# Differential attention of a transformer pair: the four raw-key projections spread over its 32 steps, and [high, low] values of 256 moving columns whose halves VectorE adds

## The chip, the cores and the metric

The kernel is one program on one NeuronCore of a Trainium2 chip, written with explicit semaphores for each engine: TensorE (PE), VectorE (DVE), ScalarE (ACT), GpSimd (POOL) and SyncE (SP). The metric is the device time of one execution in microseconds.

## The reference

Two transformer blocks over 512 tokens of width 1024 in float32. The first has a mixer and a gated feed-forward layer, the second a feed-forward layer, a mixer and another feed-forward layer. The change concerns the mixer of the second block, which has two branches over the same input `h @ w_in`:

```python
def diff_attention(q, k, v, cos, sin, lam_params, head_gain, lam_init):
    ...
        s = jnp.einsum('bqhcd,bkhcd->bhcqk', qb, k).astype(jnp.float32) * scale
        s = jnp.where(kpos[None, :] <= qpos[:, None], s, NEG_INF)
        p = jax.nn.softmax(s, axis=-1)
        a = p[:, :, 0] - lam * p[:, :, 1]
        return jnp.einsum('bhqk,bkhe->bqhe', a.astype(v.dtype), v)
    ...
    o = rmsnorm(o, head_gain) * (1.0 - lam_init)
```

with 8 heads of two 64-wide score maps and 128-wide values, and a sparse attention (`nsa`) with 16 query heads in two groups. It projects six key and value arrays. Two of them (`k_cmp`, `v_cmp`) are compressed: blocks of 32 tokens plus a position term go through a hidden layer of 256. The keys `k_slc` and `k_win` get a rotary embedding.

## The kernel before

Every float32 product is made of three passes: each operand is split into a high part (rounded to fp32r) and the rest, a low part, and `three` (L636 to L638) adds high x high, high x low and low x high in PSUM. Weights stream in 307 chunks of 128x1024 through six slots. SP loads a chunk into `raw`, ScalarE rounds it into `Wh` (L1210), VectorE subtracts for `Wl` (L1703): that pair is a *split*. It is issued five chunks ahead (`LEAD`). There are eight PSUM banks `ps[0]` to `ps[7]`, each with semaphores `full` and `free`; a table `STAGES` counts their uses in each stage. Every engine works its queue strictly in program order.

The stages around the change are, in this order: `vda` (value projection of the differential attention), `da` (the attention), `nsf` (four chunks, the feature-major projections of `k_cmp`, `v_cmp`, `k_slc` and `k_win`, called the raw keys here), `nst` (three chunks, the other values and the gates), `rope_q` (eight chunks) with the compression (`cmp`) between them, and `nsa`.

`da` has 32 steps t, four query tiles for each of 8 heads; the tile t % 4 sees (t % 4 + 1) x 128 keys. A step passes over four engines:
- TensorE `scores(t)` into two of the banks 0 to 3; VectorE `maxima(t)` (`nmx`); ScalarE `exps(t)` into `Pb` (L1371); VectorE `combine(t)`: `rr`, `gg` (L1907) and the difference of both maps in `Pb` (L1910).
- TensorE `turn(t)`: transposes into bank 4 or 5; ScalarE `high(t)` (`ATdh`, L1380); VectorE `low(t)` (`ATdl`, L1918).
- TensorE `values(t)`: for each of the t % 4 + 1 key blocks three matmuls of 128 moving columns, into bank 6 or 7 in turn; ScalarE `da_out(t)` scales it into `YD` (L1387) and frees the bank.

TensorE's order in step t is `values(t-2)`, `scores(t+2)`, `turn(t)`. ScalarE's is `da_out(t-3)`, `high(t)`, `exps(t+2)`, with the high parts of the head after the next between `high` and `exps` (V at t % 4 = 1, L1417; Q and K at t % 4 = 3, L1413). VectorE's is `combine(t)`, `low(t-1)`, `maxima(t+2)`. GpSimd subtracts for the low parts of Q, K and V (L510 to L520). The compression has two hidden layers, on TensorE in L1005, the first with weights `cw1k`, the second with `cw1v`; GpSimd makes their inputs `cA` (L566), and `cw1v` is loaded over the place of `YD` once that is stored in `y_dram`.

## Time and profile before

| | us |
|---|---|
| median of 3 runs | 2101.65 (2101.18 to 2110.67) |
| the profiled execution, its own time | 2101.01 |
| its span | 2099.2 |
| TensorE busy | 2016.0 (96%) |
| VectorE busy | 1042.3 (50%) |
| ScalarE busy | 814.6 (39%) |
| GpSimd busy | 276.5 (13%) |

The span lies inside the time; what is around it is 1.8 us. Busy time of TensorE holds modelled ends, so rates are read from the starts of matmuls. The stages stand at about 1124 to 1224 us (`da`), 1224 to 1246 (`nsf`), 1246 to 1259 (`nst`) and 1259 to 1340 (`rope_q` with the compression) from the start of the span.

### The profile page before, as it was taken

What the parts mean: (1) busy time and instruction counts of PE and PEld (TensorE: products, weight loads), DVE (VectorE), ACT (ScalarE), POOL (GpSimd) and SP (SyncE); (2) the same over time, 40 slices, a digit from 0 to 9 for tenths busy, and PEclk for the clock granted to TensorE, in tenths of its full rate; (3) what the DMA queues carried; (4) which work ended last, traced back from release to release, by engine and by line L of the source; (5) the groups of instructions that cost most, each with busy time, mean ns of one, the idle gap of its engine ahead of it and who ended that gap; (6) DMA issues with size and microseconds to landing.
All of it is one profiled execution on the core that took longest, in us unless ns stands there. A gap on an engine that the chain in (4) does not pass through costs nothing.

```text
span 2099.2 us, 25667 instructions
## 1 busy us (share of the span) xinstructions
PE 2016.0 (96%) x10244; PEld 1696.5 (81%) x10244; DVE 1042.3 (50%) x1606; ACT 814.6 (39%) x1482; POOL 276.5 (13%) x272
## 2 busy tenths in 40 slices
PE   6999999999999999999998899989899999999998
PEld 6887888888888888888887688777777888888887
DVE  5675565555353222335545766766565543222333
ACT  5442443333343222324225744455554333222322
POOL 1001000000000000000012432376763000000000
PEclk9999999999999999999998999999999999999999
DMA  5231233333223333332541043212115423332332
GB/s 192 81 101 61 100 102 101 92 99 101 92 90 102 99 100 92 99 101 81 151 130 41 1 171 120 90 31 61 46 37 180 126 80 105 96 101 92 99 100 71
DMA packets 58982, 200.13 MB, mean 95 GB/s; under 512 B 8080, under 2 KB 8112, under 8 KB 58480
## 3 DMA queue, kind: packets, MB, share of 16 engines
q1 hardware_dynamic: 53936, 178.29, 27.1%
q0 software_dynamic: 4928, 20.21, 2.7%
q8 instruction: 82, 1.34, 0.2%
q14 instruction: 36, 0.29, 0.0%
HBM read 181.16 MB, written 8.39 MB: 90 GB/s over the span
## 4 chain that ended last, share of the span: by engine, by line
PE 76%; DVE 7%; POOL 5%; ACT 5%; issue 3%; DVEq 2%; DMA 1%; POOLq 1%; SPq 0%; ACTq 0%
PE ps L636 24%; PE ps L637 24%; PE ps L638 24%; POOL PU L592 5%; DMA raw<-in_w_all 1%; DVE Wl L1703 1%; DVE XN L1743 1%; PE ps L1089 1%; DVEq L2262 1%; POOLq L581 1%; PE ps L1005 1%; ACT Pb L1371 1%; ACT Wh L1210 1%; DVE AUl L2267 1%; ACT PL L1466 1%
## 5 line engine op out<-in xcount | busy, mean ns | idle before, releaser
L1703 DVE TENSOR_TENSOR Wl<-raw,Wh 128x1024 fp32r<-128x1024 f32 x307 | 378.3, 1235 | 754.1 <-ACT Wh L1210 752.7
L636 PE MATMUL ps<-HTh,Wh 128*128 128x512 f32 (+1 forms) x1728 | 647.4, 375 | 8.9 <-DVE HTl L1752 7.0
L638 PE MATMUL ps<-HTh,Wl 128*128 128x512 f32 (+1 forms) x1728 | 641.9, 371 | 0.0
L637 PE MATMUL ps<-HTl,Wh 128*128 128x512 f32 (+1 forms) x1728 | 641.6, 371 | 0.0
L1210 ACT CAST Wh<-raw 128x1024 fp32r<-128x1024 f32 x307 | 322.0, 1051 | 782.5 <-DMA raw<-in_w_all 782.5
L636 PEld LDWEIGHTS ps<-HTh,Wh 128*128 128x128 f32 x1728 | 327.5, 190 | 64.7 <-issue 9.7
L638 PEld LDWEIGHTS ps<-HTh,Wl 128*128 128x128 f32 x1728 | 327.0, 189 | 56.1
L637 PEld LDWEIGHTS ps<-HTl,Wh 128*128 128x128 f32 x1728 | 327.3, 189 | 54.0
L636 PE MATMUL ps<-Wh,Yh 128*128 128x512 f32 x528 | 205.8, 390 | 0.0
L638 PE MATMUL ps<-Wh,Yl 128*128 128x512 f32 x528 | 205.5, 389 | 0.0
L637 PE MATMUL ps<-Wl,Yh 128*128 128x512 f32 x528 | 205.4, 389 | 0.0
L592 POOL TENSOR_SCALAR PU<-PU,ugg 128x512 f32<-128x512 f32 (+3 forms) x128 | 137.8, 1094 | 107.2 <-DVE ugg L2263 107.2
L636 PE MATMUL ps<-Wh,HTh 128*128 128x512 f32 (+2 forms) x320 | 119.1, 372 | 1.8 <-ACT qkr L1458 1.8
L637 PE MATMUL ps<-Wl,HTh 128*128 128x512 f32 (+2 forms) x320 | 118.1, 369 | 0.0
L638 PE MATMUL ps<-Wh,HTl 128*128 128x512 f32 (+2 forms) x320 | 118.1, 369 | 0.0
L638 PEld LDWEIGHTS ps<-Wh,Yl 128*128 128x128 f32 x528 | 99.1, 188 | 20.6
L636 PEld LDWEIGHTS ps<-Wh,Yh 128*128 128x128 f32 x528 | 99.1, 188 | 20.5
L637 PEld LDWEIGHTS ps<-Wl,Yh 128*128 128x128 f32 x528 | 99.1, 188 | 20.4
L1623 ACT ACTIVATE PU<-ps,umx 128x512 f32<-128x512 f32 (+3 forms) x128 | 65.7, 526 | 58.5 <-DVE umx L2255 58.5
L636 PEld LDWEIGHTS ps<-Wh,HTh 128*128 128x128 f32 x320 | 60.4, 189 | 12.0 <-ACT qkr L1458 2.2
L638 PEld LDWEIGHTS ps<-Wh,HTl 128*128 128x128 f32 x320 | 60.2, 188 | 10.1
L637 PEld LDWEIGHTS ps<-Wl,HTh 128*128 128x128 f32 x320 | 60.3, 188 | 9.7
(281 smaller groups left out, 2370.0 us busy)
## 6 DMA issues: line engine op xcount, KB each, us to landing
raw<-in_w_all SPq DMA_DIRECT2D x307, 512.0 KB, 3.5
swp_d<-qkd SPq DMA_DIRECT2D x64, 64.0 KB, 2.7
g_dram<-gst SPq DMA_DIRECT2D x16, 256.0 KB, 4.0
ring<-g_dram POOLq DMA_DIRECT2D x16, 256.0 KB, 3.5
gpre<-in_g_pre POOLq DMA_DIRECT2D x5, 512.0 KB, 3.8
X<-in_x SPq DMA_DIRECT2D x4, 512.0 KB, 5.0
swp_r<-qkr SPq DMA_DIRECT2D x16, 128.0 KB, 2.3
cw1k<-in_cw POOLq DMA_DIRECT2D x1, 2048.0 KB, 8.6
```

The source lines that it names most:

```text
L581: pool.drain()
L592: last = pool.tensor_scalar(p, p, ugg[:, s % 2, i:i + 1], None, ALU.mult)
L636: tensor.matmul(dst, a_hi, b_hi, start=start, stop=False)
L637: tensor.matmul(dst, a_hi, b_lo, start=False, stop=False)
L638: return tensor.matmul(dst, a_lo, b_hi, start=False, stop=stop)
L1005: last = tensor.matmul(ps[kv][:, ht * 64:ht * 64 + 62], cw[:, j, ht * P:(ht + 1) * P], cA[:, kv, j, :], start=j == 0, stop=j == 15)
L1089: return tensor.transpose(dst, p[:, a:a + P], ident[:])
L1210: scalar.copy(Wh[:, s, :], raw[:, s, :]).then_inc(w_hi, 1)
L1371: scalar.activation(Pb2[:, u, m, 0:w], ps[b][:, 0:w], ACT.Exp, bias=nmx[:, u, m:m + 1], accum_out=rs[:, u, m:m + 1]).then_inc(free[b], 1)
L1466: last = scalar.activation(PL[:, u, p:p + w], ps[b][:, o:o + w], ACT.Exp, bias=lmx[:, u, i:i + 1], accum_out=lsum[:, u, i:i + 1])
L1623: last = scalar.activation(PU[:, (s + 1) % 2, SCORE_AT[i]:SCORE_AT[i] + w], ps[b][:, o:o + w], ACT.Exp, bias=umx[:, s % 2, i:i + 1], accum ...
L1703: vector.tensor_tensor(Wl[:, s, :], raw[:, s, :], Wh[:, s, :], ALU.subtract).then_inc(w_lo, 1)
```

## The change

- The `nsf` stage is put ahead of `da` in the table, its 32 pieces (one `three` of 512 columns for each chunk and contraction tile) go into `da`: six ahead of the loop (`FIRST_STEPS`) and one behind `turn(t)` in the steps 0 to 25, all into bank 7. When a chunk is complete, at steps 2, 10, 18 and 26, ScalarE copies the bank (`nsf_out`) at the start of the step, and both engines make one weight split at the step's end.
- `Vst` holds the high and the low part of each key block side by side. `values` takes one matmul with 256 moving columns and one with 128 for each block, all into bank 6; the right half of the bank holds high x low. `da_out(t-2)` writes the left half to `YD`, and a new VectorE instruction `add_low(t-2)` adds the right half and frees the bank.
- The raw slice and window keys (`kraw`) and their swapped copy lie where the query tiles of finished heads were. Their swap DMAs are issued behind the last `nsf` chunk.
- TensorE no longer waits for all eight banks ahead of the loop.
- Behind the loop: squares and their reduction in two halves; the rotary work comes ahead of the head norms, and these come behind the low parts of the `nst` values. GpSimd loads `posT` and `cw1k` during `da`, makes both inputs in a row, and then stores `YD` and loads `cw1v`. The low part of the rotated keys (`ksl`) moves from c = 1 to c = 5 of `rope_q`.

```diff
-    ("da", 0, [0] * 8, [16, 16, 16, 16, 16, 16, 16, 16]),
-    ("nsf", 4, [1, 1, 1, 1, 0, 0, 0, 0], [0] * 8),
+    ("nsf", 4, [0, 0, 0, 0, 0, 0, 0, 4], [0] * 8),
+    ("da", 0, [0] * 8, [16, 16, 16, 16, 16, 16, 32, 0]),
...
-        Vst = at("Vst", -8, [P, 2, 2, SEQ], F32R)
+        Vst = at("Vst", -8, [P, 2, TT, 2, P], F32R)
...
-        DSQ = at("DSQ", 64, [P, TT, D])
+        DSQ = [at("DSQ0", 0, [P, 2, D]), at("DSQ1", 76, [P, 2, D])]
...
-        kraw = at("kraw", 44, [P, 2, SEQ])
...
+        kraw = at("kraw", 8, [P, 2, SEQ])
...
+        FIRST_STEPS = 6
+
+        def nsf_ends(t):
+
+            done = FIRST_STEPS + t
+            return done // 8 - 1 if done % 8 == 0 and 8 <= done <= 32 else None
...
-                c = m - CHUNK0["nsf"]
-                if c in (2, 3) and on("nsf"):
-                    swap("nsf", c - 2, c, 0, kraw[:, c - 2, :], swp_n[:, c - 2, :])
+                if m == CHUNK0["nsf"] + 3 and on("nsf"):
+                    for c in range(2):
+                        swap("nsf", c, 7, 2 + c, kraw[:, c, :], swp_n[:, c, :])
...
                 v_low(0, 7)
-
-                for b in (6, 7):
-                    pl.wait_ge(full[b], FILLED["nsf"][b])
+                if on("cmp"):
+                    pool.drain()
+                    load(posT[:], t["posT"], in_pos)
+                    load(cw1k[:].rearrange("p j n -> p (j n)"), t["cw1"][0], in_cw)
+
+                pl.wait_ge(full[6], FILLED["da"][6] + TOTAL)
...
-                for tt in range(TT):
-                    pl.wait_ge(da_fin, tt + 1)
-                    pl.dma_start(y_dram[tt], YD[:, tt, :]).then_inc(yd_out, 16)
                 def inputs(kv):
 
-                    pl.wait_ge(free[kv], FREED["nst"][kv])
+                    pl.wait_ge(free[7], FREED["nsf"][7] + kv + 1)
...
                 inputs(0)
+                load(w2k[:], t["w2k"], in_cw)
+                load(w2v[:], t["w2v"], in_cw)
+                inputs(1)
+                pool.drain()
+                for tt in range(TT):
+                    pl.wait_ge(da_fin, tt + 1)
+                    pl.dma_start(y_dram[tt], YD[:, tt, :]).then_inc(yd_out, 16)
                 pl.wait_ge(yd_out, 16 * TT)
                 load(cw1v[:].rearrange("p j n -> p (j n)"), t["cw1"][1], in_cwv)
-                inputs(1)
-                pool.drain()
...
             def values(t):
                 u, n = t % 2, t % 4 + 1
-                b = 6 + u
-                bank_free("da", b, t // 2)
+                b = 6
+                bank_free("da", b, t)
                 if t % 4 == 0:
                     pe.wait_ge(st_lo, 4 * (t // 4) + 4)
                 bank_free("da", 4 + u, t // 2 + 1)
                 for j in range(n):
                     a = slice(j * P, (j + 1) * P)
-                    last = three(ps[b][:, 0:P], ATdh[:, u, 0, a], ATdl[:, u, 0, a], Vst[:, t // 4 % 2, 0, a], Vst[:, t // 4 % 2, 1, a],
-                                 j == 0, j == n - 1)
+                    v = Vst[:, t // 4 % 2, j, :, :]
+                    tensor.matmul(ps[b][:, 0:2 * P], ATdh[:, u, 0, a], v.rearrange("p a n -> p (a n)"), start=j == 0, stop=False)
+                    last = tensor.matmul(ps[b][:, 0:P], ATdl[:, u, 0, a], v[:, 0, :], start=False, stop=j == n - 1)
                 last.then_inc(full[b], 1)
+
+            def nsf_steps(a, b):
+                for n in range(a, b):
+                    c, k = n // 8, n % 8
+                    w = weights(CHUNK0["nsf"] + c)
+                    if k == 0:
+                        bank_free("nsf", 7, c)
+                    q = slice(k * P, (k + 1) * P)
+                    last = three(ps[7][:], Wh[:, w, q], Wl[:, w, q], HTh[:, k, :], HTl[:, k, :], k == 0, k == KT - 1)
+                    if k == KT - 1:
+                        last.then_inc(w_used, 1)
 
             def attention():
                 scores(0)
                 scores(1)
+                nsf_steps(0, FIRST_STEPS)
                 for t in range(TOTAL):
                     if exists(t - 2):
                         values(t - 2)
                     if exists(t + 2):
                         scores(t + 2)
                     turn(t)
+                    if FIRST_STEPS + t < 32:
+                        nsf_steps(FIRST_STEPS + t, FIRST_STEPS + t + 1)
                 values(TOTAL - 2)
                 values(TOTAL - 1)
...
-                for b in range(8):
-                    pe.wait_ge(free[b], FREED["da"][b])
...
-            if on("nsf"):
-                for c in range(4):
-                    gemm_f("nsf", c, c)
...
             def da_out(t):
-                u = t % 2
-
-                if t >= TOTAL - 2:
-                    filled("da", 6 + u, t // 2)
-                scalar.activation(YD[:, t % 4, span(0, 2 * P, t // 4 * P, P)], ps[6 + u][:, 0:P], ACT.Copy,
-                                  scale=rr[:, t % STEPS, 0:1]).then_inc(free[6 + u], 1)
+                filled("da", 6, t)
+                scalar.activation(YD[:, t % 4, span(0, 2 * P, t // 4 * P, P)], ps[6][:, 0:P], ACT.Copy,
+                                  scale=rr[:, t % STEPS, 0:1]).then_inc(y_part, 1)
+
+            def nsf_out(c):
+                chunk_done("nsf", c)
+                if c >= 2:
+                    ac.wait_ge(st_lo, 4 * (4, 7)[c - 2] + 2)
+                dst = kcv[:, c, :] if c < 2 else kraw[:, c - 2, :]
+                scalar.copy(dst, ps[7][:]).then_inc(free[7], 1)
 
             def attention():
                 exps(0)
+                high_parts(0, 0, 1)
                 exps(1)
+                high_parts(0, 1, 0)
                 for t in range(TOTAL):
-                    if exists(t - 3):
-                        da_out(t - 3)
+                    if nsf_ends(t) is not None:
+                        nsf_out(nsf_ends(t))
+                    if exists(t - 2):
+                        da_out(t - 2)
                     high(t)
                     if t % 4 == 1 and exists(t + 4):
                         high_parts(0, t // 4 + 1, 1)
...
                         high_parts(0, t // 4 + 2, 0)
                     if exists(t + 2):
                         exps(t + 2)
-                for t in range(TOTAL - 3, TOTAL):
-                    da_out(t)
+                    if nsf_ends(t) is not None:
+                        split(CHUNK0["nsf"] + nsf_ends(t) + LEAD)
+                da_out(TOTAL - 2)
+                da_out(TOTAL - 1)
...
             if on("nsf"):
 
-                scalar.drain()
-                scalar.activation(DSQ[:], YD[:], ACT.Square).then_inc(da_sq, 1)
-                ac.wait_ge(da_ss, 1)
+                ac.wait_ge(free[6], FREED["da"][6] + TOTAL)
+                for n in range(2):
+                    scalar.activation(DSQ[n][:], YD[:, 2 * n:2 * n + 2, :], ACT.Square).then_inc(da_sq, 1)
+                split(CHUNK0["nst"] + LEAD)
+                ac.wait_ge(da_ss, 2)
                 scalar.activation(hsd[:], hss[:], ACT.Sqrt, scale=1.0 / P, bias=eps[:]).then_inc(da_sd, 1)
-                for c in range(4):
-                    split(CHUNK0["nsf"] + c + LEAD)
-                    chunk_done("nsf", c)
-                    dst = kcv[:, c, :] if c < 2 else kraw[:, c - 2, :]
-                    scalar.copy(dst, ps[c][:]).then_inc(free[c], 1)
             if on("nst"):
-                for c in range(3):
-                    split(CHUNK0["nst"] + c + LEAD)
+                split(CHUNK0["nst"] + 1 + LEAD)
                 chunk_done("nst", 2)
                 for tt in range(TT):
                     for m in range(2):
                         scalar.copy(vhl[m][:, tt, :, 0:HD], ps[tt][:, m * P:(m + 1) * P].rearrange("p (g d) -> p g d", g=2))
                 for tt in range(TT):
                     scalar.activation(gates[:, tt, :], ps[tt][:, 2 * P:VG_W], ACT.Sigmoid).then_inc(vs_hi, 1)
+                split(CHUNK0["nst"] + 2 + LEAD)
...
+            def add_low(t):
+
+                ve.wait_ge(y_part, t + 1)
+                y = YD[:, t % 4, span(0, 2 * P, t // 4 * P, P)]
+                vector.scalar_tensor_tensor(out=y, in0=ps[6][:, P:2 * P], scalar=rr[:, t % STEPS, 0:1], in1=y,
+                                            op0=ALU.mult, op1=ALU.add).then_inc(free[6], 1)
+
             def attention():
                 maxima(0)
                 maxima(1)
...
                     combine(t)
                     if exists(t - 1):
                         low(t - 1)
+                    if exists(t - 2):
+                        add_low(t - 2)
                     if exists(t + 2):
                         maxima(t + 2)
+                    if nsf_ends(t) is not None:
+                        split(CHUNK0["nsf"] + nsf_ends(t) + LEAD)
                 low(TOTAL - 1)
+                add_low(TOTAL - 2)
+                add_low(TOTAL - 1)
...
             if on("nsf"):
-                ve.wait_ge(da_sq, 1)
-                vector.tensor_reduce(hss[:], DSQ[:].rearrange("p i (h d) -> p (i h) d", d=P), AX.X, ALU.add).then_inc(da_ss, 1)
-                ve.wait_ge(da_sd, 1)
-                vector.reciprocal(hrs[:], hsd[:])
-                vector.drain()
-                for i in range(TT):
-                    r = hrs[:, i * 8:(i + 1) * 8].rearrange("p (h a) -> p h a", a=1).broadcast_to((P, 8, P))
-                    blk = YD[:, i, :].rearrange("p (h d) -> p h d", d=P)
-                    vector.tensor_tensor(blk, blk, r, ALU.mult).then_inc(da_fin, 1)
-                for c in range(4):
-                    split(CHUNK0["nsf"] + c + LEAD)
+                for n in range(2):
+                    ve.wait_ge(da_sq, n + 1)
+                    vector.tensor_reduce(hss[:, 16 * n:16 * n + 16], DSQ[n][:].rearrange("p i (h d) -> p (i h) d", d=P), AX.X,
+                                         ALU.add).then_inc(da_ss, 1)
+                split(CHUNK0["nst"] + LEAD)
                 ve.wait_ge(in_rope, 64)
 
                 def keys_out(kind):
...
                     last.then_inc(roped, 1)
 
                 keys_out(0)
-                split(CHUNK0["nst"] + LEAD)
+                ve.wait_ge(da_sd, 1)
+                vector.reciprocal(hrs[:], hsd[:])
+                vector.drain()
                 split(CHUNK0["nst"] + 1 + LEAD)
                 keys_out(1)
                 vector.drain().then_inc(ks_f, 1)
             if on("nst"):
-                split(CHUNK0["nst"] + 2 + LEAD)
                 for tt in range(TT):
                     ve.wait_ge(vs_hi, tt + 1)
                     for m in range(2):
                         last = vector.tensor_tensor(vhl[m][:, tt, :, HD:P], ps[tt][:, m * P:(m + 1) * P].rearrange("p (g d) -> p g d", g=2),
                                                     vhl[m][:, tt, :, 0:HD], ALU.subtract)
                     last.then_inc(free[tt], 1)
+                split(CHUNK0["nst"] + 2 + LEAD)
+                for i in range(TT):
+                    r = hrs[:, i * 8:(i + 1) * 8].rearrange("p (h a) -> p h a", a=1).broadcast_to((P, 8, P))
+                    blk = YD[:, i, :].rearrange("p (h d) -> p h d", d=P)
+                    vector.tensor_tensor(blk, blk, r, ALU.mult).then_inc(da_fin, 1)
```

Three places show how the queues change. In the rows `ps` is a bank, `Pb` the exponentials, `ATdh` and `ATdl` the two parts of the transposed weights.

TensorE, step 4, `values(2)` and the piece ahead of it; before:

```order
L789 MATMUL ps<-ident,Pb_90 128x128 x4
L636 MATMUL ps<-Vst,ATdh 128x128
L637 MATMUL ps<-Vst,ATdh 128x128
L638 MATMUL ps<-Vst,ATdl 128x128
L636 MATMUL ps<-Vst,ATdh 128x128
L637 MATMUL ps<-Vst,ATdh 128x128
L638 MATMUL ps<-Vst,ATdl 128x128
L636 MATMUL ps<-Vst,ATdh 128x128
L637 MATMUL ps<-Vst,ATdh 128x128
L638 MATMUL ps<-Vst,ATdl 128x128
```

and with the change:

```order
L795 MATMUL ps<-ident,Pb_90 128x128 x4
L642 MATMUL ps<-HTh,Wh 128x512
L643 MATMUL ps<-HTl,Wh 128x512
L644 MATMUL ps<-HTh,Wl 128x512
L808 MATMUL ps<-Vst,ATdh 128x256
L809 MATMUL ps<-Vst,ATdl 128x128
L808 MATMUL ps<-Vst,ATdh 128x256
L809 MATMUL ps<-Vst,ATdl 128x128
L808 MATMUL ps<-Vst,ATdh 128x256
L809 MATMUL ps<-Vst,ATdl 128x128
```

The third matmul of each block went into the first, and a piece of `nsf` stands between the transposes and the values.

ScalarE, step 10, where the second chunk ends; before:

```order
L1387 ACTIVATE YD<-ps,rr 128x128
L1380 CAST ATdh<-ps 128x384
L1371 ACTIVATE Pb_90,rs<-ps,nmx 128x128 x2
L1387 ACTIVATE YD<-ps,rr 128x128
L1380 CAST ATdh<-ps 128x512
```

and with the change:

```order
L1409 COPY kcv<-ps 128x512
L1401 ACTIVATE YD<-ps,rr 128x128
L1397 CAST ATdh<-ps 128x384
L1388 ACTIVATE Pb_90,rs<-ps,nmx 128x128 x2
L1227 CAST Wh<-raw 128x1024
L1401 ACTIVATE YD<-ps,rr 128x128
L1397 CAST ATdh<-ps 128x512
```

`YD` is now the output of step 8, not 7; the copy stands ahead of it, and a split behind the exponentials.

VectorE, the same step; before:

```order
L1905 RECIPROCAL rr<-rs 128x2
L1907 SCALAR_TENSOR_TENSOR gg<-rs,nlam,rr 128x1
L1910 SCALAR_TENSOR_TENSOR Pb_90<-Pb_90,gg 128x384
L1918 TENSOR_TENSOR ATdl<-ps,ATdh 128x256
L1897 TENSOR_REDUCE nmx<-ps 128x1 x2
```

and with the change:

```order
L1929 RECIPROCAL rr<-rs 128x2
L1931 SCALAR_TENSOR_TENSOR gg<-rs,nlam,rr 128x1
L1934 SCALAR_TENSOR_TENSOR Pb_90<-Pb_90,gg 128x384
L1942 TENSOR_TENSOR ATdl<-ps,ATdh 128x256
L1948 SCALAR_TENSOR_TENSOR YD<-ps,rr,YD 128x128
L1921 TENSOR_REDUCE nmx<-ps 128x1 x2
L1727 TENSOR_TENSOR Wl<-raw,Wh 128x1024
```

The addition into `YD` stands ahead of the maxima, the split behind them.

## Rows read from the trace of the kernel before

**Rows 1.** The page: busy time of each engine over the span.

```profile
PE 2016.0 (96%) x10244; PEld 1696.5 (81%) x10244; DVE 1042.3 (50%) x1606; ACT 814.6 (39%) x1482; POOL 276.5 (13%) x272
```

**Rows 2.** Windows: stretch, its length, busy of each engine, PEclk, DMA share, GB/s.

```profile
1124.00:1126.00 2.00, 1.68 (x9) 1.71 (x9) 0.29 (x1) 1.95 (x4) 1.37 (x2) 0.51 0.01 2
...
1160.00:1172.00 12.00, 9.77 (x75) 8.17 (x74) 8.84 (x24) 8.95 (x30) 5.79 (x4) 1.00 0.01 3
```

**Rows 3.** Timeline of TensorE, last value projection to first score.

```profile
1124.32 0.44 PE L636 MATMUL ps<-Kst,Qst 128*128 128x128 f32 x1 [3.38 <-DVE vd L2122]
```

**Rows 4.** Timeline of VectorE: combines at 1136 and 1219, one turn between.

```profile
1136.37 0.15 DVE L1905 RECIPROCAL rr<-rs 128x2 f32<-128x2 f32 x1
...
1159.55 0.15 DVE L1905 RECIPROCAL rr<-rs 128x2 f32<-128x2 f32 x1
...
1161.51 0.17 DVE L1905 RECIPROCAL rr<-rs 128x2 f32<-128x2 f32 x1
...
1163.94 0.15 DVE L1905 RECIPROCAL rr<-rs 128x2 f32<-128x2 f32 x1
...
1167.44 0.17 DVE L1905 RECIPROCAL rr<-rs 128x2 f32<-128x2 f32 x1 [0.60 <-ACT Pb L1371]
...
1170.07 1.51 DVE L1897 TENSOR_REDUCE nmx<-ps 128x1 f32<-128x512 f32 x2 [1.38 <-PE ps L781]
...
1171.50 0.15 DVE L1905 RECIPROCAL rr<-rs 128x2 f32<-128x2 f32 x1
...
1219.19 0.17 DVE L1905 RECIPROCAL rr<-rs 128x2 f32<-128x2 f32 x1
```

**Rows 5.** Timeline of ScalarE in the same turn.

```profile
1164.04 0.58 ACT L1380 CAST ATdh<-ps 128x512 fp32r<-128x512 f32 x1 [1.04 <-PE ps L789]
...
1166.33 0.47 ACT L1371 ACTIVATE Pb<-ps,nmx 128x256 f32<-128x256 f32 x1
...
1167.24 0.36 ACT L1387 ACTIVATE YD<-ps,rr 128x128 f32<-128x128 f32 x1
```

**Rows 6.** Timeline of TensorE in the same turn.

```profile
1162.61 0.28 PE L637 MATMUL ps<-Kst,Qst 128*128 128x256 f32 x1
...
1162.73 0.28 PE L638 MATMUL ps<-Kst,Qst 128*128 128x256 f32 x1
...
1163.39 0.61 PE L789 MATMUL ps<-ident,Pb 128*128 128x128 f32 x4
...
1168.38 0.28 PE L636 MATMUL ps<-Vst,ATdh 128*128 128x128 f32 x1
...
1168.49 0.28 PE L637 MATMUL ps<-Vst,ATdh 128*128 128x128 f32 x1
```

**Rows 7.** Timelines of VectorE and GpSimd at the same instant.

```profile
1133.75 1.28 DVE L1907 SCALAR_TENSOR_TENSOR gg<-rs,nlam,rr 128x1 f32<-128x1 f32 x1
1133.75 1.26 POOL L520 TENSOR_TENSOR Vst<-vd,Vst 128x512 fp32r<-128x512 f32 x1 [3.70 <-ACT Vst L1417]
```

**Rows 8.** Timeline of TensorE: first `nsf` and first `nst` matmul.

```profile
1224.04 0.44 PE L636 MATMUL ps<-HTh,Wh 128*128 128x512 f32 x1
...
1245.90 0.30 PE L636 MATMUL ps<-Wh,HTh 128*128 128x304 f32 x1
```

**Rows 9.** Timelines of ScalarE and VectorE: the two halves of one split.

```profile
1241.54 1.05 ACT L1210 CAST Wh<-raw 128x1024 fp32r<-128x1024 f32 x1 [2.78 <-DMA raw<-in_w_all]
...
1242.63 1.23 DVE L1703 TENSOR_TENSOR Wl<-raw,Wh 128x1024 fp32r<-128x1024 f32 x1 [2.13 <-ACT Wh L1210]
```

**Rows 10.** Timelines of VectorE and GpSimd after the attention.

```profile
1228.35 4.42 DVE L2127 TENSOR_REDUCE hss<-DSQ 128x32 f32<-128x4096 f32 x1 [5.82 <-ACT DSQ L1552]
...
1247.71 8.88 POOL L566 TENSOR_TENSOR cA<-kcv,posT 64x248 f32<-64x248 f32 x8 [8.67 <-issue]
```

**Rows 11.** The chain that ended last: start, length, what.

```profile
1270.37 7.09 PE ps L1005 x64
...
1293.40 7.14 PE ps L1005 x64
```

44 lines of the change are left out of this document (21 added, 23 removed).

## The prediction

> **What bounds the kernel now.** I read the page first: TensorE is busy for 96% of the span [rows 1], so a change pays by what it takes out of TensorE's stream or out of its waits. Next the windows and the timelines of the differential attention (1124 to 1224 us). Here TensorE is not the bound. The work goes in 32 steps, one for each query tile of each head; four steps, one head, I call a turn. A turn in the middle of the stage takes 1171.50 - 1159.55 = 11.95 us (third tile to third tile), and the seven turns from the `combine` of the first head's fourth tile to that of the last head take 1219.19 - 1136.37 = 82.8 us [rows 4]. TensorE is busy for 9.77 of 12 us [rows 2]. VectorE waits for ScalarE's exponentials (0.60) and for scores (1.38), ScalarE for transposes (1.04) [rows 4, 5]: a ring of short waits over three engines. After it TensorE runs dense: the four chunks of `nsf` take 1245.90 - 1224.04 = 21.9 us [rows 8].
>
> **What the change removes.** All 96 `nsf` matmuls leave the stretch behind the attention: -21.9 us, if they fit into TensorE's gaps there. By matmul starts, a 128-column matmul costs 0.11 (1168.38 to 1168.49) and a 256-column one 0.12 (1162.61 to 1162.73) [rows 6]; so a [high, low] pair in one matmul saves 0.10 to 0.11 for each of 80 blocks, about 8.5 us of TensorE. Per turn TensorE is busy for 9.77 us at most [rows 2], some of that modelled tails. Less 1.0 (ten blocks), plus four `nsf` steps of 21.9/32 = 0.68, that is 11.5 or less: it still fits into 11.95. Trainium skill, "TensorE: Matmul & The Clock Gate", section "Back-to-back issue gap", gives N/2.4 + 2.5 ns, that is 56 and 109 ns, and by it the pair would save 3 ns; the rows' 0.11 at 128 columns speaks against this. By the page a TensorE-bound loop would gain 8 us less; my sum has another bound and would stay.
>
> **The new loop, one turn.** VectorE gets four adds (`add_low`; I take 0.30 each, between a 128-column multiply-add from SBUF, 0.27, and a 128-column subtraction from PSUM, 0.28, plus a semaphore). ScalarE's order changes: `da_out(t-2)` now waits for the values of its own step, and VectorE's `add_low` behind it stands ahead of `maxima(t+2)`. Take 0 as the start of `combine` of the fourth tile.
> (a) Transposes at 1.35 (before: 1.88, 1163.39 [rows 6]). ScalarE's `high` 0.65 later, at 2.0; then 0.48 for it and 1.81 for the Q and K casts (1164.04 to 1166.33 is 2.29), 0.91 for the exponentials (1166.33 to 1167.24) [rows 5]: 5.2. `da_out`, 0.36: 5.6.
> (b) VectorE is there earlier: 2.43 (1161.51 to 1163.94 [rows 4]) + 0.28 + 1.46 for the next `combine` and `low` = 4.2. It waits 1.4 us. Then add 0.3 and maxima over 384 columns (1.43 for 512; I take 1.15): the next `combine` at 7.05, where it is 5.93 (1167.44) before [rows 4].
> (c) Values of the fourth tile need that add (one output bank now instead of two), start at 5.95, take 1.0; scores follow; the maxima over 512 columns start at 8.6 and take 1.43 (1170.07 to 1171.50): `combine` at 10.05, before 9.99 [rows 4]. So far nothing is lost.
> (d) ScalarE casts V at 9.26, GpSimd takes its low part from 9.96 to 11.2. VectorE's `gg` comes 0.23 into its `combine`, at 10.28, while that runs. The one place before where both start together shows `gg` at 1.28 us instead of 0.22, as long as GpSimd's 1.26 [rows 7]: an instruction with two SBUF inputs waits for GpSimd. In the middle turns of before VectorE is just ahead of it and GpSimd is the one that waits. Here VectorE loses 0.8 to 0.9. (Trainium skill, "GPSIMD Engine Reference", section "Specifications": SBUF interfaces are shared with VectorE for instructions with two SBUF inputs. By that rule the wait comes again in each turn, as the trace has it.)
> (e) `low` ends at 12.4; add 0.3, maxima over 128 columns 0.57: the next turn begins at 13.3, not 11.95: +1.35. Without (d) it is 12.4, since the exponentials end at 11.1 and `da_out` at 11.5.
> (f) At steps 2, 10, 18 and 26 a chunk ends. ScalarE adds a copy (0.5, [rows 5] has 0.58 for a 128x512 cast) and, behind the exponentials of step t+2, a split of 1.05; VectorE's half, 1.23, waits for it [rows 9]. Exponentials can begin at 13.0 after the first maximum, end 13.75; split to 14.8, VectorE's half to 16.05. Such a turn costs 16.05, that is 2.75 more. The cover is TensorE's own work, which is shorter.
> (g) From step 3 to step 31 there are three turns of 13.3, three of 16.05, and a last one without Q, K and V casts, 10.35 (VectorE's own work; before 9.89): 98.4 us, before 82.8. So +15.6.
>
> **Its start and end.** TensorE starts a score at 1124.32 after waiting 3.38 us for the last of VectorE's V copies [rows 3]; the change waits for each bank alone, so it starts when the first of four copies of 0.6 is done, 2.4 earlier, at 1121.95. But six `nsf` steps (4.1 us) now stand ahead of `scores(2)`, which VectorE's queue needs: second `combine` at 1129.9, third 1132.6, hit by (d), then the first split: fourth at 1138.8, before 1136.37 [rows 4]. +2.4. From the last `combine` to the last value it is 4.65 (before 1224.04 - 1219.19 = 4.85): -0.2.
>
> **Behind the attention.** T is the new end, 1136.37 + 2.4 + 98.4 + 4.65 = 1241.85. TensorE gets to the first hidden layer (cw1k) at T + 24.5 and to the second (cw1v) at T + 47.5, as 1270.37 and 1293.40 lie to 1245.90 [rows 8, 11]. VectorE: squares by ScalarE end T + 4.8 (halves of 3.63), reduction in two halves (4.42 in one [rows 10]) T + 7.4, split T + 9, keys 7 us under GpSimd's work T + 16, split, second keys T + 23, first bank free T + 23.5. One us of margin: I charge 0.5. GpSimd: a drain ahead of its first input instruction waits for loads in flight (8.67 us before [rows 10]), here the two rope loads, T + 5; two input stages of 8.9 [rows 10] and two loads between them: T + 26.5. VectorE's four head norms (as many elements as the 4.42 us reduction; I take 4.6) end at T + 31; y_dram lands 6.6 later and cw1v 8.5 after that, by the trace's median landing times of the same loads: T + 46.2, hidden by about 1 us. What is late next when the margin is gone is cw1v, 1 us for 1 us. The swap DMAs of the keys now sit in SP's queue behind the load for step 26, long before they are needed; rope_q swaps need `roped` 25 and 26, T + 16 and T + 23, and block only a load that isn't wanted before T + 40. The ksl subtraction (2.28) moves to c = 5, into 1.1 us of idle before `cmp_shift(1)` and 0.7 of the second score half: nothing.
>
> **Sum.** -21.9 (nsf) + 2.4 (start) + 15.6 (turns) - 0.2 (end) + 0.5 (bank) = -3.6. The profiled execution took 2101.0 us (span 2099.2), 0.65 under the median of 2101.65. 2101.0 - 3.6 = 2097.4; I say 2097.5.
>
> **Rivals.** (A) The forecast, gain of the overlap eaten by the longer turns: 2092 to 2101, chance 0.5.
> (B) The turns keep the length of before, and only the splits lengthen them by VectorE's own 1.2: T = 1138.0 + 82.8 + 3.6 + 4.65 = 1229, that is 2084. If VectorE's work alone bounds (11.95 less 0.60, 1.38 and 0.23 of waits, plus 1.2 for the adds, and 1.2 per split), T is near 1222 and the time 2077. For it: that idle time [rows 4]. Against: the waits in (b) and (f) come out of queue order, not load. Chance 0.17.
> (C) Collisions as in (d) do not happen, because the V cast falls elsewhere: 7 x 0.9 less, 2091. Chance 0.1, half of it under 2091.
> (D) The other side: GpSimd's Q and K lows (three instructions of 1.27 us from 3.2 on) also hit `combine` of the first two tiles. In my schedule these hide behind the 1.4 us wait of (b). If that wait is under 0.5 us, each turn pays 0.8 to 1.3: +6 to +9, 2103 to 2106. Chance 0.13.
> (E) The granted clock. Behind the 3.38 us of idle it stood at 0.51 [rows 2], 1.2 instead of 2.4 GHz. The change leaves 1.2 us of idle there and dense work behind it, so I expect 1.0. If it falls anyway, the six steps cost 4 us more and each further us at the low level up to 0.5: 2102 to 2113. Chance 0.07.
> (F) cw1v or the keys are late by several us: 2100 to 2105, chance 0.03.
>
> **How the numbers follow.** What a measurement here can tell from no change is about 0.5%, 10.5 us: faster is below 2091.1. Faster: all of B, half of C and a little of A = 0.24. Slower, above 2112.2: the tail of E and D, 0.03. Same: 0.73. The range leaves out the lower half of B and the upper end of E: 2084 to 2106. Unknown costs lie in it: an add of 0.25 or 0.4 (32 x 0.05 to 0.1, 2 to 3 us), (d) between 0 and 1.27 per turn (-6 to +3).
>
> **What the new profile would show.** `nst` starts at 1242 (right: 1237 to 1247; B right: before 1230). `combine` of a fourth tile to the next: 13.3 and, with a chunk's end, 16.0. VectorE idle before `add_low`, released by ScalarE's YD, near 1.4 per turn, and before the split's Wl near 2. `gg` of third tiles at about 1 us. PEclk 1.0 throughout the attention. No TensorE wait at the first hidden layer over 1 us. The prediction is wrong if ScalarE gets to `da_out` before VectorE asks for it, or if TensorE waits for cw1v.

## The result

The changed kernel takes 2117.8 us (median; 2116.3 to 2120.2, 7 runs), the kernel before 2101.65: a ratio of 1.0066 (95% interval 1.0051 to 1.0081), 0.66% slower. The forecast was 2097.5, with 2084 to 2106 as its range. It was wrong in sign and size. Single executions of the kernel before go from 2100.9 to 2110.7 us and those of the changed one from 2116.3 to 2120.2, so the two don't overlap. The profiled execution has a span of 2116.0 us where that of before has 2099.2: 16.8 us to find.

The page of the changed kernel says little. TensorE is busy 10 us longer than in [rows 1] with 80 instructions fewer, so part of its work ran slower; PEclk in 40 slices of 53 us shows where:

```profile
PE 2026.0 (96%) x10164; PEld 1704.8 (81%) x10164; DVE 1052.2 (50%) x1639; ACT 816.1 (39%) x1483; POOL 275.2 (13%) x272
...
PEclk9999999999999999999999987999999999999999
```

**The attention came out near the forecast, in part by luck.** VectorE's timeline of one turn with a split; the reciprocals are `combine`'s first instruction, as in [rows 4]:

```profile
1157.22 0.35 DVE L1948 SCALAR_TENSOR_TENSOR YD<-ps,rr,YD 128x128 f32<-128x128 f32 x1 [1.58 <-ACT YD L1401]
...
1161.23 0.15 DVE L1929 RECIPROCAL rr<-rs 128x2 f32<-128x2 f32 x1
...
1161.74 1.57 DVE L1934 SCALAR_TENSOR_TENSOR Pb<-Pb,gg 128x384 f32<-128x384 f32 x1
...
1166.12 1.23 DVE L1727 TENSOR_TENSOR Wl<-raw,Wh 128x1024 fp32r<-128x1024 f32 x1 [1.68 <-ACT Wh L1227]
1167.26 0.16 DVE L1929 RECIPROCAL rr<-rs 128x2 f32<-128x2 f32 x1
```

One line shows the wait of (b): before its add into `YD` VectorE stood 1.58 us for ScalarE's `da_out`. (d) is there too, but it fell on `Pb`, 1.57 us where the same form elsewhere takes 0.62, and only in three of the six turns that prepare a V: in the other three GpSimd's instruction was the one that took longer (1.71 us instead of 1.27). Before its half of the split (`Wl`) it stood 1.68 us for ScalarE's half. The eight fourth-tile combines are at 1138.63, 1151.59, 1167.26, 1181.84, 1197.51, 1210.52, 1226.17 and 1237.84: 99.2 us where 98.4 were forecast. Single turns were off by -0.4 to +1.3 us, and the errors partly cancelled.

Two things of the attention were missed: TensorE waits up to 2.98 us for `Pb` behind a split, and its granted clock falls behind such waits. Timeline, then windows (PEclk is the third number from the end):

```profile
1168.96 1.12 PE L795 MATMUL ps<-ident,Pb 128*128 128x128 f32 x4 [2.98 <-DVE Pb L1934]
```

```profile
1160.00:1170.00 10.00, 5.96 (x41) 5.18 (x40) 7.62 (x18) 5.39 (x15) 1.27 (x1) 0.91 0.20 56
1170.00:1180.00 10.00, 10.00 (x52) 8.18 (x50) 6.37 (x18) 6.65 (x18) 4.22 (x4) 0.75 0.00 0
```

Even so TensorE reached the first hidden layer at 1269.80, ahead of the 1270.37 of [rows 11], and did not wait there. **All of the loss, and 0.6 us more, lies behind that point.** What TensorE did from 1284 on, in its timeline:

```profile
1287.97 0.39 PE L644 MATMUL ps<-HTh,Wl 128*128 128x512 f32 x1
1293.87 7.09 PE L1051 MATMUL ps<-kcb,qn 128*128 128x64 f32 x32 [5.51 <-ACT qn L1608]
1300.75 13.86 PE L1021 MATMUL ps<-cA,cw1v 128*128 128x62 f32 x64
```

It stood 5.51 us for ScalarE's `qn` (`query(3)`), where the kernel before stands 0.69:

```profile
1289.62 3.79 PE L1035 MATMUL ps<-kcb,qn 128*128 128x64 f32 x32 [0.69 <-ACT qn L1585]
```

Then the 32 matmuls of `cmp_scores(0)` took 7.1 us (before: 3.8) and the second hidden layer 13.6 from its start to the next stage (before: 7.1). The clock was at its lower level, 1.2 GHz (PEclk 0.50):

```profile
1284.00:1290.00 6.00, 4.36 (x20) 3.25 (x18) 0.00 (x0) 0.00 (x0) 0.00 (x0) 1.00 0.91 365
1292.00:1316.00 24.00, 22.13 (x100) 21.84 (x101) 7.12 (x10) 6.44 (x7) 0.60 (x1) 0.50 0.10 27
```

ScalarE's timeline says what held `query(3)`, and the DMA issues say why (line, queue, count, KB of one, median us to landing):

```profile
1282.96 0.41 ACT L1603 COPY kcb<-ps 64x62 f32<-64x62 f32 x2
1292.15 1.04 ACT L1227 CAST Wh<-raw 128x1024 fp32r<-128x1024 f32 x1 [8.78 <-DMA raw<-in_w_all]
1293.22 0.60 ACT L1608 ACTIVATE qn<-ps 128x512 f32<-128x512 f32 x1
```

```profile
1281.98 0.54 POOL L471 DMA_DIRECT2D cw1v<-in_cw  x1 [6.71 <-DMA y_dram<-YD]
```

```profile
1282.46 0.33 SPq L450 DMA_DIRECT2D raw<-in_w_all  x1
```

```profile
cw1v<-in_cw POOLq DMA_DIRECT2D x1, 2048.0 KB, 9.7
raw<-in_w_all SPq DMA_DIRECT2D x2, 512.0 KB, 7.7
```

ScalarE's order is split, then query. The split waited 8.78 us for a weight chunk, issued at 1282.46 and used at 1292.15, 9.7 us later; the page's median landing of a chunk is 3.5. GpSimd had issued the 2 MB load of cw1v half a microsecond ahead of it, at 1281.98, after 6.71 us for the stores of YD. The DMA share from 1284 to 1290 is 0.91. The kernel before has cw1v issued at 1256.55. Its ScalarE waits for the same chunk too, but 3.47 us:

```profile
1287.41 1.05 ACT L1210 CAST Wh<-raw 128x1024 fp32r<-128x1024 f32 x1 [3.47 <-DMA raw<-in_w_all]
1288.97 0.60 ACT L1585 ACTIVATE qn<-ps 128x512 f32<-128x512 f32 x1 [0.51 <-PE ps L638]
```

Its query then still waits 0.51 us for TensorE: half a microsecond was all the margin of that queue, and I had not looked at it. By the starts of TensorE's rows up to 1340, the changed kernel loses 4.8 us by the longer wait, 3.3 and 6.5 us in the two slow stages, and 1.9 in the first projection matmuls behind them, at 0.43 instead of 0.23: 16.4. About 1 us more is lost behind 1500 us, where its clock is below 1.0 for longer than that of before.

### The profile page after: what moved, and what is told of

Read it like the earlier page. It is cut to its first block, busy times and chain, and to the rows that moved or that the text cites. A ratio compares the mean times of both kernels' runs of the same rounds, so it can differ in the third digit from the quotient of the medians.

```text
span 2116.0 us, 25539 instructions
## 1 busy us (share of the span) xinstructions
PE 2026.0 (96%) x10164; PEld 1704.8 (81%) x10164; DVE 1052.2 (50%) x1639; ACT 816.1 (39%) x1483; POOL 275.2 (13%) x272
## 3 DMA queue, kind: packets, MB, share of 16 engines
q8 instruction: 81, 1.33, 0.2%
## 4 chain that ended last, share of the span: by engine, by line
PE 75%; DVE 7%; POOL 5%; ACT 5%; issue 3%; DVEq 2%; DMA 2%; POOLq 1%; SPq 0%; ACTq 0%
PE ps L642 23%; PE ps L644 23%; PE ps L643 23%; POOL PU L598 5%; DMA raw<-in_w_all 2%; PE ps L1021 1%; DVE XN L1767 1%; ACT Wh L1227 1%; PE ps L1105 1%; DVE Wl L1727 1%; DVEq L2300 1%; ACT XN L1260 1%; POOLq L587 1%; DVE AUl L2305 1%; ACT PL L1495 1%
```

## The experiments

Theory 1: a chain. cw1v slows a chunk, ScalarE's split waits, `query(3)` is queued behind it, TensorE waits, its clock falls. Every ratio below is to the kernel before, whose median on the chips of these runs was 2104.4 to 2105.9 us.

### query_first: query ahead of the split from c = 3 on

```diff
                 for c in range(8):
-                    split(CHUNK0["rope_q"] + c + LEAD)
+                    if c < 3:
+                        split(CHUNK0["rope_q"] + c + LEAD)
                     query(c)
+                    if c >= 3:
+                        split(CHUNK0["rope_q"] + c + LEAD)
```

> The changed kernel (2117.8 us), with one move on ScalarE: from query(3) on, query(c) stands ahead of the split of the weight chunk and no longer behind it. No engine does more or less. Theory 1 (the loss of 16 us is a chain: the 2 MB load of cw1v slows a weight chunk from 3.5-4.3 to 9.67 us, ScalarE's split waits for it, query(3) is queued behind, TensorE stands 5.5 us and its clock then stays at half until 1318): the load still overlaps the chunk and the chunk still takes over 8 us, but the wait of TensorE ahead of cmp_scores(0) falls from 5.51 to under 1.5 us, the clock stays at 1.0, hidden layer 2 starts by 1293 instead of 1300.95, and the kernel takes 2100 to 2103 us. Rival A (TensorE would only wait later, at hidden layer 2 for cw1v itself, which lands at 1291.7): a wait of 3 to 5 us there, clock down again, 2110 to 2115. Rival B (the loss has its root in the attention, where the clock fell already): no change, 2116 to 2119.

2107.4 us, ratio 1.0016 (0.9999 to 1.0032): 5 of 6.6 thousandths regained, not all, and more than the 2100 to 2103 us expected. The wait is 0.69 us, the second hidden layer starts at 1292.5: the chain up to there is as theory 1 has it. But a new wait stands at the next attention:

```profile
1336.30 0.79 PE L1094 MATMUL ps<-ksh,QSn 128*128 128x512 f32 x1 [3.84 <-ACT PU L1650]
```

```profile
1306.99 1.23 DVE L1730 TENSOR_TENSOR Wl<-raw,Wh 128x1024 fp32r<-128x1024 f32 x1 [6.29 <-ACT Wh L1227]
...
1333.32 1.19 DVE L2239 TENSOR_TENSOR CS<-CS,cst 128x992 f32<-128x992 f32 x1
```

VectorE's half of a split now waits 6.29 us for ScalarE's half behind `query(4)`, and VectorE's later work, the scores' shift that ScalarE's exps need, comes 5 us later (1333.32, in query3 below 1328.15; 1.9 us of that is a head start that query3's execution has since the attention). I had moved the queue's mistake from one engine to another.

### filled_gap: TensorE kept busy in the gap

```diff
                 rope_q(3)
+                bank_free("cmpa", 3)
+                for n in range(24):
+                    tensor.matmul(ps[3][:], HTh[:, n % 8, 0:P], HTh[:, n % 8, :], start=True, stop=True)
                 pe.wait_ge(free[7], FREED["rope_q"][7] + 2)
```

> The changed kernel with 24 matmuls of 512 columns more on TensorE behind rope_q(3), whose results nobody reads (bank 3 is free there). They fill the 5.5 us for which TensorE waits; ScalarE's order, the load and the chunk stay. It parts the wait from the clock. Theory 1 says that of the loss of 16 to 17 us the wait itself is 4.8 and the halved clock behind it 11 to 12: with the gap filled the clock stays at 1.0, cmp_scores(0) takes 3.8 and hidden layer 2 takes 7.1 us as in the kernel before, and the kernel takes 2105 to 2108 us. Rival C (the clock falls because of what ran before the gap, or the load, and not because of the gap): the clock is at half all the same and the kernel takes 2116 to 2121.

2104.8 us, ratio 1.0003 (0.9989 to 1.0017). The forecast of theory 1 was 2105 to 2108. The chunk was as late as before, and idle work alone gave back 13 us (1 us of it, by the traces, is a head start that this execution has at the first hidden layer):

```profile
1291.46 1.05 ACT L1230 CAST Wh<-raw 128x1024 fp32r<-128x1024 f32 x1 [9.14 <-DMA raw<-in_w_all]
```

```profile
1293.00:1304.00 11.00, 10.81 (x97) 10.81 (x97) 6.46 (x9) 3.73 (x4) 0.00 (x0) 1.00 0.10 25
```

The granted clock stayed at 1.00, and rival C falls. So of the loss the larger part is the clock, not the wait.

### no_transfer: without cw1v's load

The load is left out, and the second hidden layer takes the weights of the first.

```diff
-                load(cw1v[:].rearrange("p j n -> p (j n)"), t["cw1"][1], in_cwv)
...
-                    cw = (cw1k, cw1v)[kv]
+                    cw = cw1k
```

> The changed kernel without the load of cw1v: hidden layer 2 uses cw1k instead and waits for the stores of YD alone, so its values are not the reference's. Theory 1: the weight chunk that took 9.67 us takes 3.5 to 4.5, ScalarE's split and query(3) come 5 us earlier, TensorE waits under 1 us, the clock stays at 1.0, and the kernel takes 2100 to 2103 us, the same as with query(3) ahead. Rival D (the chunk is slow for another reason, such as being requested late): the chunk still takes over 7 us and the time stays at 2112 to 2119.

2110.4 us, ratio 1.0013 (0.9990 to 1.0035). ScalarE's wait for the chunk fell from 8.78 to 4.38 us and TensorE's from 5.51 to 1.11: the chunk lands 5.3 us after its issue instead of 9.7, so the load is what slows it (rival D falls; 3.5 to 4.5 had been expected). But behind a wait of 1.11 us the clock fell all the same and stood at 0.50 from 1291 to 1311 in this execution:

```profile
1288.85 5.21 PE L1050 MATMUL ps<-kcb,qn 128*128 128x64 f32 x32 [1.11 <-ACT qn L1607]
```

```profile
1287.13 1.05 ACT L1226 CAST Wh<-raw 128x1024 fp32r<-128x1024 f32 x1 [4.38 <-DMA raw<-in_w_all]
```

The time expected of it, 2100 to 2103, was missed by the median and by the profiled run (2109.1 us of span). The ten runs lie in two groups: four at 2100.4 to 2103.0, as expected, and six at 2110.4 to 2113.8. In the profiled one, of the second group, TensorE takes 9.7 us more than before from `cmp_scores(0)` to `cmp_scores(1)`. That the first group are the executions in which the clock holds would fit, but none of them was profiled.

### norms_early: stores and cw1v earlier

The four products are also taken out behind the lows of `vhl`.

```diff
                 vector.reciprocal(hrs[:], hsd[:])
                 vector.drain()
+                for i in range(TT):
+                    ...
+                    vector.tensor_tensor(blk, blk, r, ALU.mult).then_inc(da_fin, 1)
```

> The changed kernel with VectorE's four products of the head norms put back ahead of the keys (as the kernel before has them) instead of behind the lows of vhl. YD is stored and cw1v loaded some 10 us earlier (issue by 1272 instead of 1281.98). Theory 1: the load falls on another chunk, one that no queue is waiting for; TensorE's wait at cmp_scores(0) falls below 1.5 us and the clock holds; but the norms (4 x 1.1 us) now delay the keys and the vhl lows, which may cost TensorE up to 3 us at the first hidden layer: 2100 to 2106 us. Rival E (wherever the load lies it hits the chunk that ScalarE waits for, since a chunk is asked for every 3 us): a wait of 3 to 5 us appears at an earlier chunk, 2110 to 2118.

2114.1 us, ratio 1.0048 (1.0028 to 1.0067). The norms moved the wait to VectorE's side: TensorE stood at the first hidden layer for the lows of `vhl`, and the layer took 13.3 us:

```profile
1271.62 13.27 PE L1021 MATMUL ps<-cA,cw1k 128*128 128x62 f32 x64 [3.77 <-DVE vhl L2196]
```

cw1v was issued at 1278.66, only 3.3 us earlier, since the stores wait on GpSimd behind `inputs(1)`; the issue by 1272 that I expected did not come. At `cmp_scores(0)` the wait was 0.69. The time lies in the range of rival E, but by another path than E's: the wait is for VectorE, as theory 1 had allowed with up to 3 us, and no chunk was in flight beside cw1v. So this run says little on where the load could stand.

### query3: the one query that matters

```diff
-                    split(CHUNK0["rope_q"] + c + LEAD)
-                    query(c)
+                    if c == 3:
+                        query(c)
+                        split(CHUNK0["rope_q"] + c + LEAD)
+                    else:
+                        split(CHUNK0["rope_q"] + c + LEAD)
+                        query(c)
```

> As query_first, but only query(3) stands ahead of its split; for query(4) to query(7) the split is ahead again. In query_first the wait at cmp_scores(0) was gone (0.7 us, clock 1.0, hidden layer 2 at 1292.5), and a new one of 3.8 us stood at the first scores of the next attention (1331 to 1335), after which the clock was at half. Theory 1 with this added (a split that waits for its chunk delays whatever stands behind it; the moved splits now stood ahead of the next attention's exps): that wait goes back to 0.6 us, no fall of the clock up to 1344, and the kernel takes 2098 to 2101 us, no more than the kernel before. Rival F (the wait at 1331 comes from elsewhere in the changed kernel, such as the later keys): it stays, and the time is that of query_first, 2105 to 2108.

2103.8 us, ratio 1.0003 (0.9991 to 1.0014). Two instructions exchanged give back the 0.66%. `cw1v` still takes 9.4 us, the chunk beside it 8.1, and ScalarE still waits for it, but the query is no longer behind it:

```profile
1287.01 3.79 PE L1051 MATMUL ps<-kcb,qn 128*128 128x64 f32 x32 [0.69 <-ACT qn L1608]
```

```profile
1286.36 0.60 ACT L1608 ACTIVATE qn<-ps 128x512 f32<-128x512 f32 x1 [5.03 <-PE ps L644]
1288.58 1.04 ACT L1227 CAST Wh<-raw 128x1024 fp32r<-128x1024 f32 x1 [1.62 <-DMA raw<-in_w_all]
```

The time is 3 us over what I expected; the kernel before, on these chips, is 3 us over its first median too. Theory 1 stands: with the chain cut, the changed kernel equals the one before. One thing doesn't add up in the medians: filled_gap keeps the wait of 4.8 us and query3 doesn't, yet both measure 1.0003. The traces say more. query3 is 2.6 us ahead of before at 1322 and until 1530; then its clock falls where that of before doesn't, at a wait of the same length, and it ends level. First query3, then before, TensorE and its windows:

```profile
1533.24 2.40 PE L1105 MATMUL ps<-ident,PU 128*128 128x128 f32 x10 [3.36 <-POOL PU L598]
1530.00:1545.00 15.00, 11.76 (x59) 9.84 (x59) 6.12 (x15) 7.08 (x23) 9.33 (x10) 0.77 0.13 39
```

```profile
1535.32 1.31 PE L1089 MATMUL ps<-ident,PU 128*128 128x128 f32 x10 [3.35 <-POOL PU L592]
1530.00:1545.00 15.00, 11.50 (x73) 9.47 (x72) 8.05 (x21) 7.53 (x23) 11.11 (x11) 1.00 0.18 47
```

Now the question is the one that the forecast answered with -3.6: where do the 21.9 us go that leave the stretch behind the attention?

### query3_lag: the split's halves in different steps

```diff
 ScalarE
-                    if nsf_ends(t) is not None:
-                        split(CHUNK0["nsf"] + nsf_ends(t) + LEAD)
+                    if nsf_ends(t - 1) is not None:
+                        split(CHUNK0["nsf"] + nsf_ends(t - 1) + LEAD)
 VectorE
-                    if nsf_ends(t) is not None:
-                        split(CHUNK0["nsf"] + nsf_ends(t) + LEAD)
+                    if nsf_ends(t - 2) is not None:
+                        split(CHUNK0["nsf"] + nsf_ends(t - 2) + LEAD)
```

> query3, and in the attention each split of a weight chunk stands one step later on ScalarE and two steps later on VectorE, so that VectorE never waits for ScalarE's half of it. In the changed kernel the turns with a split took 15.67 us against 13.0, and the split itself is only 1.05 and 1.23 us; TensorE stood 2.98 us and its clock fell. Theory 2 (the split's excess over its 1.2 us is the two engines' halves in one step, and the gap that drops the clock): split turns take 14.2 to 14.8, four of them save 4 to 6 us, and the kernel takes 2093 to 2097 us. Rival G (the halves are cheap and what is slow in a turn is the chain exps, da_out, add_low, maxima): under 1.5 us, 2097 to 2100.

2096.2 us, ratio 0.9968 (0.9951 to 0.9985). Turns with a split take 14.4 us (1164.91 to 1179.28; the first 14.5), the others 13.0; the last combine is at 1231.78, in query3 at 1235.81. Time and turns are as theory 2 has them. VectorE's waits ahead of `Wl` in the loop (6.9 us in query3) are gone, TensorE's longest for `Pb` from 3.0 to 1.8, and PEclk was 1.00 from 1120 to 1220. A split now costs a turn 1.4 us more, near VectorE's own 1.2 for it.

### old_values and old_values_lag: values as in the kernel before

```diff
-                    tensor.matmul(ps[b][:, 0:2 * P], ATdh[:, u, 0, a], v.rearrange("p a n -> p (a n)"), start=j == 0, stop=False)
-                    last = tensor.matmul(ps[b][:, 0:P], ATdl[:, u, 0, a], v[:, 0, :], start=False, stop=j == n - 1)
+                    last = three(ps[b][:, 0:P], ATdh[:, u, 0, a], ATdl[:, u, 0, a], v[:, 0, :], v[:, 1, :], j == 0, j == n - 1)
...
-                    if exists(t - 2):
-                        add_low(t - 2)
```

> query3 with the values as three products of 128 columns, as in the kernel before: ScalarE's da_out frees the bank and VectorE adds no halves; the key projections stay inside the attention, the values' bank stays single. It undoes one part of the change. Per head that gives VectorE back four add_low (0.3 us each and their waits, 16.6 us in 15 over the loop) and costs TensorE ten matmuls of 0.11 us. Theory 3 (VectorE's add_low and its wait for da_out, queued behind ScalarE's exps, set the turn): the loop's 99.2 us fall by 6 to 12, and the kernel takes 2088 to 2094 us. Rival H (TensorE's own work sets the turn, since the projections take their place in it): the added 8.8 us of matmuls take it back, 2098 to 2104.

> old_values and the later splits together. By theory 2 and 3 the two savings add but for 1 to 2 us: 2084 to 2091. If the turn is then set by TensorE's own work (rival H), the later splits give under 2 us on top of old_values.

old_values: 2100.5 us, ratio 0.9993 (0.9972 to 1.0014). From the first to the last of the fourth-tile combines it takes 95.1 us, query3 98.0: 2.9 us less, not 6 to 12. The time is in the range of rival H, but what held it wasn't TensorE's work alone: VectorE's waits for `da_out` (15.2 us in 13 over query3's loop) became waits for scores (16.7 us in 14) and for ScalarE's half of the splits (10.4 us in 4; 6.9 in query3). With the splits apart (old_values_lag) it pays: 2088.8 us, 0.9918 (0.9900 to 0.9935) in 4 runs, against 0.9968 of query3_lag, combines in steps of 12.1 and 14.8 us, the last at 1228.04.

### values_alone: the other part, on the kernel before

```diff
-                    last = three(ps[b][:, 0:P], ATdh[:, u, 0, a], ATdl[:, u, 0, a], Vst[:, t // 4 % 2, 0, a], Vst[:, t // 4 % 2, 1, a],
-                                 j == 0, j == n - 1)
+                    v = Vst[:, t // 4 % 2, j, :, :]
+                    tensor.matmul(ps[b][:, 0:2 * P], ATdh[:, u, 0, a], v.rearrange("p a n -> p (a n)"), start=j == 0, stop=False)
+                    last = tensor.matmul(ps[b][:, 0:P], ATdl[:, u, 0, a], v[:, 0, :], start=False, stop=j == n - 1)
...
+                    if exists(t - 3):
+                        add_low(t - 3)
```

> The kernel before with one part of the change alone: values as 256 and 128 moving columns, the right half added by VectorE at step t-3, two banks as before; the key projections stay behind the attention. TensorE saves ten matmuls per head; VectorE gains four add_low of 0.34 us per head. Theory 3 (VectorE and ScalarE set the turn, TensorE does not): the saved matmuls buy nothing and each turn of 11.95 us grows by 0.3 to 1.4 us, 2 to 11 us over eight heads: 2104 to 2113 us where the kernel before has 2102 to 2105. Rival H (TensorE's work sets the turn): the turn falls by up to 1 us, 2094 to 2101.

2111.5 us, ratio 1.0030 (1.0019 to 1.0041). Its seven turns take 1225.95 - 1135.05 = 90.9 us, in [rows 4] 82.8: the part costs 8 us, though it takes 8 us of matmuls out of TensorE. Waits of the attention (us in all, times, longest):

```profile
PE ps L789 <- DVE Pb L1912: 14.4, 9, 1.9
DVE YD L1926 <- ACT YD L1388: 13.0, 8, 2.3
PE ps L802 <- DVE YD L1926: 10.8, 8, 2.0
```

In the kernel before TensorE waits 6.6 us for `Pb` and 9.0 for the values' banks, and VectorE has no add to wait for. The part is a loss by itself. It costs 8 us here, 5 thousandths in query3_lag and 1 thousandth, within the noise, in query3, where VectorE's waits for the split's other half took its place.

### nst_early, scores_first and nst_early_filled: more out of the end

On top of old_values_lag, the first `nst` chunk goes into the attention's end, then scores ahead of values, then (on nst_early alone) ten idle matmuls ahead of the first hidden layer:

```diff
 nst_early
+                nst_tiles(0, (0, 1))
                 values(TOTAL - 2)
+                nst_tiles(0, (2, 3))
                 values(TOTAL - 1)
 scores_first
-                    if exists(t - 2):
-                        values(t - 2)
                     if exists(t + 2):
                         scores(t + 2)
+                    if exists(t - 2):
+                        values(t - 2)
 nst_early_filled
                 rope_q(1)
+                bank_free("cmpa", 4)
+                for n in range(10):
+                    tensor.matmul(ps[4][:], HTh[:, n % 8, 0:P], HTh[:, n % 8, :], start=True, stop=True)
                 cmp_hidden(0)
```

> old_values_lag with the first chunk of the next projection (nst, 36 matmuls of 304 columns, 5 us, banks 0 to 3, which the last exps have freed) inside the attention's end: tiles 0 and 1 ahead of values(30), tiles 2 and 3 ahead of values(31). There TensorE stood some 2 us in waits and ran at half clock from 1229 to 1240. Theory 4 (the end of the attention is a gap that costs itself and the clock behind it; work that is ready fills it): the first hidden layer starts 3 to 6 us earlier than in old_values_lag (1261.8), clock 1.0 at 1230 to 1240, 2083 to 2087 us. Rival I (behind the attention VectorE's reductions, splits and lows set the time, not TensorE): the first hidden layer waits for the lows of vhl or cm_a as much longer, under 1 us gained.

> nst_early with scores(t + 2) ahead of values(t - 2) on TensorE. In old_values_lag VectorE's maxima wait 13.8 us over the loop for scores, which stand behind the values. If that wait sits in the turn's chain (scores, maxima, exps, da_out, high), the loop shortens by 3 to 8 us: 2076 to 2083. Rival J (da_out and with it the values' bank then come later, and what was saved at the maxima is lost at values): within 1.5 us of nst_early, or slower.

> nst_early with ten matmuls of 512 columns more on TensorE ahead of the first hidden layer, whose results nobody reads (bank 4): they last about the 2.25 us for which TensorE there waits for the lows of vhl. In nst_early the first hidden layer started 3.6 us earlier than in old_values_lag but took 10.9 us in place of 6.9, and at the next attention all was lost (1322.9 against 1320.0). Theory 5 (what is won ahead of a wait is lost because the wait halves the clock behind it; the wait itself loses nothing): the first hidden layer starts at 1258 to 1259 and takes 7.0 us, the clock holds, the next attention starts at 1315 to 1317, 2084 to 2088 us. Rival K (what stands behind, the stores of YD, cw1v or the chunks, then sets the time): a wait of over 1 us turns up at the second hidden layer or at cmp_scores(0), clock down there, 2091 to 2097.

nst_early 2096.5 us (0.9965, 0.9949 to 0.9981), scores_first 2097.2 (0.9968, 0.9952 to 0.9985), nst_early_filled 2100.7 (0.9979, 0.9967 to 0.9990): all three worse than the 2088.8 they build on. In scores_first the loop took 89.9 us instead of nst_early's 91.0, not 3 to 8 less, and the time is the same (rival J). TensorE's timelines of nst_early and of nst_early_filled:

```profile
1258.17 11.37 PE L1026 MATMUL ps<-cA,cw1k 128*128 128x62 f32 x64 [2.25 <-DVE vhl L2197]
```

```profile
1258.24 7.33 PE L1026 MATMUL ps<-cA,cw1k 128*128 128x62 f32 x64 [0.58 <-DVE vhl L2200]
...
1283.54 13.42 PE L1026 MATMUL ps<-cA,cw1v 128*128 128x62 f32 x64 [2.02 <-DMA cw1v<-in_cw]
```

In nst_early the layer starts 3.6 us earlier than in old_values_lag, after 2.25 us of wait for VectorE's lows (rival I), and takes 10.9 us at a falling clock. The wait is one that the edit made: `values(31)` now stands behind the tiles, ScalarE's last `da_out` and the squares behind it come 4.9 us later than in best_again (the last section of these), and VectorE's lows end at 1259.2 instead of 1256.4. ScalarE, first nst_early, then best_again:

```profile
1236.63 0.37 ACT L1406 ACTIVATE YD<-ps,rr 128x128 f32<-128x128 f32 x1 [3.49 <-PE ps L644]
```

```profile
1231.74 0.37 ACT L1400 ACTIVATE YD<-ps,rr 128x128 f32<-128x128 f32 x1 [1.65 <-PE ps L644]
```

And the 3.6 us are against an execution whose clock had fallen at the attention's end. best_again, the same kernel, starts the layer at 1255.92, without a wait. Filled, the wait is 0.58 and the layer takes 7.1 us, as theory 5 has it; but then TensorE is at the second hidden layer before cw1v has landed, waits 2.02 us, and that layer takes 13.4 us at half clock (rival K; the time, 2100.7, is above K's 2091 to 2097 too). What TensorE wins ahead of VectorE and the loads becomes a wait, and in these two each such wait cost the layer behind it 4 to 6 us.

### best_again: old_values_lag once more

> old_values_lag unchanged, a second time: its first median, 2088.8 us, rests on 4 runs. By the traces (first hidden layer 8.4 us ahead of the kernel before, 6.9 us left at the end of the span) a ratio of 0.993 to 0.997 is expected, 2089 to 2097 us; rival L (the first ratio of 0.9918 holds): under 2089.

2088.5 us (2086.1 to 2091.6, 6 runs), ratio 0.9925 (0.9910 to 0.9940): rival L, just. This kernel, the projections inside the attention, values as before, splits one and two steps later, `query(3)` ahead of its split, is 0.75% faster than the kernel before and 1.4% faster than the changed one. The two profiled executions of this kernel differ by 7.3 us of span: 1.4 are there before the attention's loop, 4.4 come at its end, the rest later. The end, first of this run and then of old_values_lag:

```profile
1228.00:1240.00 12.00, 11.54 (x85) 11.29 (x86) 6.95 (x6) 7.68 (x9) 4.92 (x7) 1.00 0.28 89
```

```profile
1228.00:1240.00 12.00, 11.30 (x53) 10.72 (x52) 4.65 (x8) 6.62 (x9) 1.61 (x3) 0.58 0.14 46
```

## Why the prediction was wrong

**What bounds the kernel:** right. The attention is bound by short waits over three engines: taking 8 us of matmuls out of TensorE made it slower (values_alone, which gives VectorE 32 adds for them), and moving the splits by a step or two made it 3.7 us faster (query3_lag), with no work taken out.

**The loop, (a) to (g):** the sum was right within 1 us, 99.2 against 98.4, and so were the waits of (b) and (f): 1.58 and 1.68 against 1.4 and 2. The sum is in part luck. Three turns with a split took 15.67, 15.67 and 15.65 (forecast 16.05), the others 12.96, 13.01 and, with the clock at 0.77, 14.58 (13.3), the last 11.67 (10.35). (d) was to cost each of the first six turns 0.9: it came in the three with a split alone, cost 0.95 there and hit `Pb`, not `gg`. In the other three rival (C) was right about the collision, but two of these turns took 13.0 and one 14.58, not the 12.4 that (e) has without it.

**The start and the end:** the start was right, +2.3 where +2.4 was forecast, and TensorE began at 1121.70 (1121.95), after 1.07 us of wait and with the clock at 1.0. The end was mis-sized. From the last combine to `nst` it was 6.2 us (1237.84 to 1244.05), not 4.65, since `values(31)` ran at half clock and waited 0.84 for `add_low(30)`.

**"PEclk 1.0 throughout the attention", rival (E):** wrong. I looked only at the one long wait at the start. Behind the waits that my own (f) makes longer, up to 2.98 us, the clock was at 0.75 to 0.95 in seven of the twelve windows of 10 us from 1120 to 1240. In query3_lag, where no wait of TensorE in the loop was over 1.6 us until 1230, it was 1.00 from 1120 to 1220.

**"Behind the attention":** the step that failed. "What is late next when the margin is gone is cw1v, 1 us for 1 us" weighed the load by its landing alone, against the second hidden layer. In the changed kernel it never was late there: TensorE came at 1300.75, and it had landed at 1291.7. It hurt by what it did to another transfer: a chunk that takes 4.4 us in the kernel before (5.3 in no_transfer) took 9.7, and ScalarE's split, `query(3)` and TensorE stood in line behind it. I had the issue time right within 1 us (T + 37.7 forecast, 1281.98 for a T of 1244.05) and did not ask which chunk is on its way then. And 1 us for 1 us was wrong by the clock: 4.8 us of wait cost 16.4. The sum had no term for this chain at all. Rival (F), "cw1v or the keys are late by several us", 0.03, had the right load with the wrong mechanism and a small part of the price.

**Sum:** up to the first hidden layer -3.6 was the forecast and -0.6 the outcome. The 3 us between are 1.6 at the end of the attention, 1.3 in the projections behind it, which began at the lower clock, and 0.8 in the turns, less 0.5 that was charged for a bank and 0.1 at the start. In query3, with the same attention, it was -2.6, so executions of one program differ by 2 us here; the time of that kernel is that of before (1.0003). That the two parts belong together I took for granted: the values part costs 8 to 9 us alone, and without it the projections inside the attention, with the splits moved, bring 0.75% (best_again) where both parts bring 0.32% (query3_lag).

**Left open:** why the same kernel's clock falls at the attention's end in one execution and not in the next; why a 3.35 us wait left the clock alone in one kernel and a 3.36 us wait didn't in the next; and whether the loop's collision with GpSimd, never taken away here, is worth the 0.95 us that it takes in three turns.

## What to carry to other kernels

When a change moves a large load, don't ask only when it lands: ask which small transfer is in flight beside it, which engine waits for that one first, and what is queued behind. Price a wait of the engine that sets the time by the clock behind it as well: here the clock cost 11.6 us behind a wait of 5.51 us and 9.7 behind one of 1.11, so the price doesn't shrink with the wait. And since the clock may fall or hold from one execution to the next, compare medians of many runs, and traces from a common point on. Split work that two engines do in turn should stand in different steps (query3_lag), and a split that may wait for a transfer behind the work that another engine needs soon (query3).

## What the runs showed of the chip

At the two hidden layers and `cmp_scores(0)`, waits of TensorE of 0.44 to 0.69 us left the granted clock at 1.0 (2.4 GHz) in the traces shown; waits of 1.11, 2.02, 2.25, 3.77 and 5.51 us there were followed by 0.50 (1.2 GHz) for 14 to 27 us of dense work, and that of 3.84 us in query_first by 7 us. It is no law: waits of 1.33 and 0.24 us at the attention's end gave 0.58 in one execution and 1.00 in another, and 3.36 and 3.35 us at 1530 gave 0.77 in query3 and 1.00 in the kernel before. Matmuls whose result nobody reads held the clock (filled_gap: 13 us won by 5.5 us of idle work). The Trainium skill, "TensorE: Matmul & The Clock Gate", section "HAM oscillation — how this bites in real kernels", describes the same mechanism, an engine that waits for data between its matmuls and goes on at half clock; these rows agree. The gaps that it warns of are longer than the 1.11 to 2.25 us that were enough in three traces here.

A 2 MB load beside a 512 KB chunk stretched the chunk to 9.7 us, from 5.3 in no_transfer and 4.4 in the kernel before. The load itself took 9.7 us, 8.5 in the kernel before; loads of its size take 8.0 to 11.1 in the runs here, so whether the chunk slowed it isn't shown.
